# Weight halves made once in block 0 of a decoder step, kept in DRAM, and loaded by the later blocks

## What is computed

```python
h = rmsnorm(x, attn_norm_g)
z = h @ w_in                                   # one projection, split into q,k,v,iq,ik,iw,gq,gk,gv,gr,glr
score = sum_h iw[h] * relu(iq[h] . ik)         # indexer; each query keeps its top-k keys
_, sel = top_k(where(admissible, score, -inf), topk)
a_o = softmax(q . k[sel] / 8 + rel_bias) @ v[sel]
g_o = gated_linear_attention(gq, gk, gv, glr)  # chunked, with its own norm and gate
x = x + concat(a_o, g_o) @ w_out
h = rmsnorm(x, ffn_norm_g)
x = x + (silu(h @ w_gate) * (h @ w_up)) @ w_down
y = rmsnorm(x, final_norm_g)
```

## Time and profile before

| | PE | DVE | ACT | POOL |
|---|---|---|---|---|
| busy us | 3274.2 | 2305.7 | 1701.0 | 1621.3 |
| share | 82% | 58% | 43% | 41% |

### The profile page before, as it was taken

How to read it: one execution, slowest core, us unless ns; L and a number is a source line. 1 busy time by engine, 2 the same in 40 slices (tenths; PEclk the granted TensorE clock), 3 DMA queues, 4 the chain that set the end, 5 groups by cost and what they waited for, 6 DMA issues and landing times.

```text
span 4000.7 us, 56701 instructions
## 1 busy us (share of the span) xinstructions
PE 3274.2 (82%) x19950; PEld 1877.7 (47%) x19950; DVE 2305.7 (58%) x4243; ACT 1701.0 (43%) x2557; POOL 1621.3 (41%) x1232
## 2 busy tenths in 40 slices
PE   4972598899979988999189988999287867899865
PEld 1451346344456543444176543444066653344455
DVE  3625762689934645999843646999977430300155
ACT  0332232554455336544164335644064434554356
POOL 1015200567662035676042034576120113676524
PEclk9995696999989999999599989999699867999856
DMA  2301031223321311233010311233010144233356
GB/s 84 94 25 43 6 99 50 65 95 98 96 86 33 97 66 62 85 93 97 0 64 28 101 58 60 73 96 98 18 35 1 36 159 151 79 97 93 101 190 224
DMA packets 112098, 313.51 MB, mean 78 GB/s; under 512 B 14034, under 2 KB 20514, under 8 KB 111746
## 3 DMA queue, kind: packets, MB, share of 16 engines
q1 hardware_dynamic: 111874, 310.63, 24.6%
HBM read 296.35 MB, written 14.24 MB: 78 GB/s over the span
## 4 chain that ended last, share of the span: by engine, by line
PE 53%; DVE 25%; issue 6%; DMA 4%; ACT 3%; POOLq 3%; DVEq 2%; POOL 2%; PEldq 0%; SPq 0%; ACTq 0%; PEld 0%
PE bank L606 12%; PE bank L607 12%; PE bank L608 12%; DVE spare L1435 11%; PE bank L870 5%; PE bank L859 2%; DVE cand L1451 2%; DVE scores L1491 2%; DVE miss L1448 2%; DVE ring L1405 2%; DMA kT<-in_w_gu 1%; DVE R L1779 1%; POOL H L2063 1%; ACT ring L1059 1%; DVE spare L1470 1%
## 5 line engine op out<-in xcount | busy, mean ns | idle before, releaser
L606 PE MATMUL bank<-H,ring 128*128 128x512 f16 (+2 forms) x2560 | 852.9, 350 | 104.3 <-POOL H L2063 52.9
L607 PE MATMUL bank<-H,ring 128*128 128x512 f16 (+2 forms) x2560 | 853.0, 350 | 0.0
L608 PE MATMUL bank<-H,ring 128*128 128x512 f16 (+2 forms) x2560 | 852.8, 350 | 0.0
L1435 DVE TENSOR_SCALAR_CACHE_REDUCE spare<-scores,cand 128x640 uint8<-128x640 f32 (+8 forms) x448 | 662.3, 1478 | 40.5 <-issue 0.9
L1902 POOL TENSOR_TENSOR ring<-raw,ring 128x1024 f16<-128x1024 f32 (+1 forms) x216 | 407.9, 1895 | 283.2 <-ACT raw L1061 277.5
L1059 ACT ACTIVATE ring<-raw 128x1024 f16<-128x1024 f32 (+2 forms) x356 | 348.7, 980 | 371.0 <-DMA raw<-in_w_d 150.8
L606 PEld LDWEIGHTS bank<-H,ring 128*128 128x128 f16 (+1 forms) x2560 | 257.9, 102 | 370.6 <-issue 101.2
L1405 DVE SCALAR_TENSOR_TENSOR ring<-raw,ring 128x1024 f16<-128x1024 f32 x140 | 198.9, 1424 | 307.7 <-ACT ring L1059 306.7
L608 PEld LDWEIGHTS bank<-H,ring 128*128 128x128 f16 (+1 forms) x2560 | 259.6, 102 | 246.1 <-issue 7.4
L607 PEld LDWEIGHTS bank<-H,ring 128*128 128x128 f16 (+1 forms) x2560 | 258.7, 102 | 236.0 <-issue 4.3
L845 PE MATMUL bank<-kT,q 128*128 128x256 f16 (+3 forms) x384 | 128.8, 340 | 278.6 <-DVE mx L1779 249.6
(11 more groups left out here) (307 smaller groups left out, 6119.8 us busy)
## 6 DMA issues: line engine op xcount, KB each, us to landing
raw<-in_w_gu SPq DMA_DIRECT2D x132, 512.0 KB, 3.6
raw<-in_w_in SPq DMA_DIRECT2D x104, 512.0 KB, 3.5
kT<-in_w_gu SPq DMA_DIRECT2D x88, 512.0 KB, 3.8
raw<-in_w_d SPq DMA_DIRECT2D x48, 384.0 KB, 3.2
X<-in_xT SPq DMA_DIRECT2D x8, 2048.0 KB, 9.1
raw<-in_w_d SPq DMA_DIRECT2D x48, 320.0 KB, 3.4
raw<-in_w_out SPq DMA_DIRECT2D x24, 512.0 KB, 3.7
kT<-in_w_d SPq DMA_DIRECT2D x32, 384.0 KB, 3.2
```

The costliest lines, as they stand in the source:

```text
L606: mm(o, lhs[0], rhs[0], start=first, stop=False)
L607: mm(o, lhs[0], rhs[1], start=False, stop=False)
L608: return mm(o, lhs[1], rhs[0], start=False, stop=last)
L1435: v.tensor_scalar(flags[:, 0:128 * (i + 1)], row_of(i), cut_at[:, i % 4:i % 4 + 1], None, ALU.is_ge, ALU.add, accum_out=tally[:, i % 4:i % ...
```

## The change

P0, O0, U0 and D0 split their weights as before (split_here), but SP stores each pair of halves to a DRAM buffer, split_w, of 107 tiles; a pair of float16 halves has as many bytes as the float32 tile. The save of tile n−2 is issued ahead of the load of tile n, behind the same wait for "w_split", and the last two tiles of P0 and of D0 are saved at the end of the stage (save_rest). highs waits for the save of the tile that had its ring slot before. All tiles of P1 to P4 and of O, U and D in F1 to F4 are loaded from split_w straight into the ring: SP waits for "products" of the tile that had the slot, and PE waits for the load. ACT and the lows of DVE and POOL skip these tiles. There are four slots as before, and from the fifth tile of P4 on eight, the other four in kT. F4's eight O tiles are all loaded in A4 (two before). The U loop of F3 and F4 runs in turns of eight tiles. The diff, cut; left out are the constants, the counting helpers loads_of and saved counts, the index argument added to the other calls of weights, and the U loop on PE, which only follows the turns:

```diff
+        split_w = nc.dram_tensor("split_w", (NW, 128, 2, WT), F16, kind="Internal").ap()
...
+        def split_here(n):
+
+            return n < W_O or base["O", 0] <= n < base["P", 2]
+
+        def raw_no(n):
+
+            return n if n < W_O else n - base["O", 0] + W_O
+
         def raw_at(n):
-
-
-            last = base["P", NBLK] + 4
-            if n < last:
-                return raw[:, n % 2, :], S(f"weights_in{n % 2}"), n // 2, 2
-            m = (n - last) % 4
-            keys = kT[:, :, :, :].rearrange("p g s n -> p (g s n)").bitcast(F32)
-            return keys[:, WT * m:WT * m + WT], S(f"last_weights_in{m}"), (n - last) // 4, 4
+            r = raw_no(n)
+            return raw[:, r % 2, :], S(f"weights_in{r % 2}"), r // 2
+
+        EIGHT = base["P", NBLK] + 4
+        late_ring = kT[:, :, :, :].rearrange("p g s n -> p (g s n)").rearrange("p (m s n) -> p m s n", m=4, s=2)
+
+        def slot_of(n):
+
+            return n % 4 if n < EIGHT or n % 8 < 4 else 4 + n % 4
+
+        def ring_at(n):
+
+            return (ring if slot_of(n) < 4 else late_ring)[:, n % 4, :, :]
+
+        SLOT_USERS = [[n for n in range(at) if slot_of(n) == m] for m in range(8)]
+        USE = {n: k for users in SLOT_USERS for k, n in enumerate(users)}
+
+        def user_before(n):
+
+            k = USE[n]
+            return SLOT_USERS[slot_of(n)][k - 1] if k else None
+
+        def turns(n):
+
+            return 4 if n < EIGHT else 8
...
+            def saved_at(w, i, step):
+
+                if i is None:
+                    return split_w[w]
+                return split_w[bass.ds(i * step + w, 1)].rearrange("t p s m -> p (t s) m")
+
+            def save(n, w, cols, i=None, step=0):
+
+                sp.dma_start(saved_at(w, i, step)[:, :, 0:cols], ring[:, n % 4, :, 0:cols]
+                             ).then_inc(S(f"w_saved{n % 4}"), 16)
+
+            def save_rest(n, w, cols):
+
+                for d in range(2):
+                    sp.wait_ge(S("w_split"), raw_no(n + d) + 1)
+                    save(n + d, w + d, cols[d])
+                for m in range(4):
+                    sp.wait_ge(S(f"w_saved{m}"), 16 * saves_of(n + 1 - (n + 1 - m) % 4))
+
+            def weights(n, src, w, i=None, step=0, saved_cols=WT):
                 cols = src.shape[-1]
-                place, arrived, m, places = raw_at(n)
-                if m:
-
-                    sp.wait_ge(S("w_split"), value(n - places + 1, i, step))
-                sp.dma_start(place[:, 0:cols], src).then_inc(arrived, 16)
+                if split_here(n):
+                    r = raw_no(n)
+                    if r >= 2:
+
+                        sp.wait_ge(S("w_split"), value(r - 1, i, step))
+                    if r >= 2 and r not in (W_O, W_O + 1):
+                        save(n - 2, w - 2, saved_cols, i, step)
+                    place, arrived, _ = raw_at(n)
+                    sp.dma_start(place[:, 0:cols], src).then_inc(arrived, 16)
+                else:
+                    if user_before(n) is not None:
+                        sp.wait_ge(S("products"), value(user_before(n) + 1, i, step))
+                    sp.dma_start(ring_at(n)[:, :, 0:cols], saved_at(w, i, step)[:, :, 0:cols]
+                                 ).then_inc(S(f"halves_in{slot_of(n)}"), 16)
...
+                    if b == 0:
+                        save_rest(W_O - 2, W_O - 2, (WT, WT))
...
-                    for t in range(2):
-                        weights(base["O", b] + t, a["w_out"][t])
+                    for t in range(KT):
+                        weights(base["O", b] + t, a["w_out"][t], W_O + t)
...
+                    turn = turns(base["U", b])
+
+                    def gate_up_weights(count, i=None):
+
+                        for r in range(count):
+                            f = (0 if i is not None else 2 * NF // turn * turn) + r
+                            if i is None:
+                                row = a["w_gu"][f // 2]
+                            else:
+                                row = a["w_gu"][bass.ds(i * (turn // 2) + r // 2, 1)].rearrange("t p m -> p (t m)")
+                            weights(base["U", b] + f, row[:, WT * (r % 2):WT * (r % 2) + WT], W_U + f, i, turn)
+
+                    with sp.Fori(0, 2 * NF // turn) as i:
+                        gate_up_weights(turn, i)
+                    gate_up_weights(2 * NF % turn)
...
+                    if b == 0:
+                        save_rest(base["P", 2] - 2, NW - 2, [128 * len(D_BLOCKS[r]) for r in (2, 3)])
...
-                pe.wait_ge(S("w_split"), value(n + 1, i, step))
-                return ring[:, n % 4, 0, :], ring[:, n % 4, 1, :]
+                if split_here(n):
+                    pe.wait_ge(S("w_split"), value(raw_no(n) + 1, i, step))
+                else:
+                    pe.wait_ge(S(f"halves_in{slot_of(n)}"), value(16 * loads_of(n), i, 16 * step // turns(n)))
+                w = ring_at(n)
...
-                whole, arrived, m, places = raw_at(n)
-                act.wait_ge(arrived, value(16 * (m + 1), i, 16 * step // places))
+                if not split_here(n):
+                    return
+                whole, arrived, m = raw_at(n)
+                act.wait_ge(arrived, value(16 * (m + 1), i, 16 * step // 2))
                 if n >= 4:
                     act.wait_ge(S("products"), value(n - 3, i, step))
+                if saves_of(n) > 1:
+                    act.wait_ge(S(f"w_saved{n % 4}"), value(16 * (saves_of(n) - 1), i, 16 * step // 4))
                 last = A(ring[:, n % 4, 0, 0:cols], whole[:, 0:cols], ACT.Copy, scale=W_UP)
...
             def lows(n, i=None, step=0, cols=WT):
-                dve.wait_ge(S("w_high"), value(n + 1, i, step))
+                if not split_here(n):
+                    return
+                dve.wait_ge(S("w_high"), value(raw_no(n) + 1, i, step))
...
-                if kind == "F" and b == NBLK:
-                    with dve.Fori(0, NF // 2 - 1) as i:
-                        for r in range(4):
-                            lows(base["U", b] + 4 + r, i, 4)
-                    for r in range(ND):
-                        lows(base["D", b] + r, cols=128 * len(D_BLOCKS[r]))
-                    with dve.Fori(0, KT - 1) as i:
-                        for r in range(ND):
-                            lows(base["D", b] + ND + r, i, ND, 128 * len(D_BLOCKS[r]))
...
-                pool.wait_ge(S("w_high"), value(n + 1, i, step))
+                if not split_here(n):
+                    return
+                pool.wait_ge(S("w_high"), value(raw_no(n) + 1, i, step))
```

More of the change, by code:

```diff
@@ L472, in _ @@
                             phase_start(sp, nph)
-                        weights(n0 + t, a["w_in"][t] if t < len(TILES) else a["w_out"][t - len(TILES)])
+                        weights(n0 + t, a["w_in"][t] if t < W_O else a["w_out"][t - W_O], t)
                         if t == 18 and b < NBLK:
@@ L553, in _ @@
                         load_x(b, NT)
-                    for t in range(4 if woven(b) else 2, KT):
-                        weights(n0 + t, a["w_out"][t])
-                    with sp.Fori(0, NF // 2) as i:
-                        for r in range(4):
-                            row = a["w_gu"][bass.ds(i * 2 + r // 2, 1)].rearrange("t p m -> p (t m)")
-                            weights(base["U", b] + r, row[:, WT * (r % 2):WT * (r % 2) + WT], i, 4)
+                    for t in range(4 if woven(b) else 2 if b < NBLK else KT, KT):
+                        weights(n0 + t, a["w_out"][t], W_O + t)
+                    turn = turns(base["U", b])
[10 more added lines that the diff above has]
+                    gate_up_weights(2 * NF % turn)
                     with sp.Fori(0, KT // 2) as i:
@@ L565, in _ @@
                             ks = D_BLOCKS[r % ND]
-                            weights(base["D", b] + r, row[:, 128 * ks[0]:128 * ks[-1] + 128], i, 2 * ND)
+                            weights(base["D", b] + r, row[:, 128 * ks[0]:128 * ks[-1] + 128], W_D + r, i, 2 * ND,
+                                    WT if r < 2 else 128 * len(D_BLOCKS[(r - 2) % ND]))
+                    if b == 0:
+                        save_rest(base["P", 2] - 2, NW - 2, [128 * len(D_BLOCKS[r]) for r in (2, 3)])
                     if b + 2 <= NBLK:
                         for t in range(2):
-                            weights(base["P", b + 2] + t, a["w_in"][t])
+                            weights(base["P", b + 2] + t, a["w_in"][t], t)
                     if b == NBLK - 1:
@@ L994, in _, with up_tiles @@
                     pe.wait_ge(S("f_h"), KT * (b + 1))
-                    def gate_up_loop():
-                        with pe.Fori(0, NF // 2) as i:
-                            for r in range(4):
-                                w = weights_at(base["U", b] + r, i, 4)
-                                pe.wait_ge(S("u_bank_free"), i * 4 + (u0 + r + 1))
-                                for k in range(KT):
```

(20 more changed lines are left out.)

19 lines of the change are left out of this document (13 added, 6 removed).

## The result

The changed kernel takes 3788.11 us (median of four, 3777.9 to 3798.9) against 4003.95 before (median of four); the ratio is 0.945 [0.940, 0.950].

A forecast was written before the change was run, and what follows sets the result against it. Bounds: PE in 512-column matmul stages, DVE's search tail before A2 and A3, and block 4's matmuls and waits for halves. Terms −73 − 47 + 15.5 + 4 − 25 − 38 = −163.5; 4002.9 − 163.5 − 0.5 = 3839 us, range 3805 to 3885.

The forecast's parts named there:

- if PE alone is the bound: Block 4's U4 and D4: the far end of that term, PE's 81 us setting the length, −49 us.
- The search: F1 and F2: without POOL's lows DVE's top-k search steps are no longer stretched, −73 us; ends 30 and 95.
- Rival 2: F1 and F2: POOL's other instructions take over the collisions, the two stages give 30; 3882 us, chance 0.10.
- The lows in the A stages: A0 to A3: DVE's lows waiting for ACT's highs no longer hold up attention, −47 us; ends −25 and −68.
- The saves: Block 0: saves ahead of loads cost +15.5 us, at the start, O0 and D0; ends +5 and +34.
- Rival 3: Block 0: a load moves only after the save before it has landed; 3909 us, chance 0.08.
- The wait in G2 and G3: G2 and G3: store o_v goes out later and POOL waits for it, +4 us; ends 0 and +10.
- O1 and O2, P4, and the way into F3: Lows and splits there go: −2.5 us in each of F1 and F2, −10 in P4, −10 into F3; −25.
- Block 4's F: F4: halves load straight into eight places at 346 GB/s, U4 and D4 −33 us, O4 and A4 −5; −38.
- rival 1: F4 is already at the DMA rate it can have, 265 GB/s; 3865 us, chance 0.15.
- Rival 4: Blocks 1 to 3: with only four ring slots, slow loads of halves hold up PE; 4069 us, chance 0.04.
- Rival 5: Whole kernel: halves are saved but stages stay as long, within 0.2% of before; chance 0.01.

The follow-up runs named there:

- again: The changed kernel, unaltered, measured and profiled once more: 3780.27 us (3775.9 to 3787.1), ratio 0.943 against before.
- a_splits: The changed kernel, with ACT and DVE splitting four tiles of constant data again in each of A1 to A3: whole execution 3812.86 us.
- best: The changed kernel plus early store o_v, block 0 loads ahead of saves, and D tile halves side by side: 3755.38 us, 0.937 against before.
- pool_busy: The changed kernel, with POOL again running an instruction of the old lows' shape on an unneeded buffer in F1 and F2: whole execution 3885.91 us.
- late_store: The kernel before, with store o_v in P2 and P3 made to wait for the product of P's last tile: ratio 0.999 [0.998, 1.001].
- four_slots: The changed kernel with four ring slots to the end instead of eight, four of O4's tiles loaded in A4: whole execution 3814.85 us.

## Why the prediction was wrong

Its mechanisms stood where they were tested, and no term had the wrong sign in both profiles. The spans of the two profiles are 203.6 and 218.6 us shorter than before, so the sum of 163.5 is short by 40 and by 55: nearly every gain was sized short, and some stages were put at nothing.

**The step that failed: PE's own time was held fixed.** The sum took away waits and instructions and left each matmul its old duration, and so it put stages such as G1 at nothing. But for the same matmuls PE's busy time over the whole span fell from 3274 us to 3226, and to 3210 in again, and with it the mean granted clock rose from 0.887 to 0.910 and 0.918. In A3 it rose from 0.91 to 0.95, 8 us less of PE, undone by a_splits with the stops. In G1, put at nothing, it rose from 0.53 to 0.77 and the stage fell by 12.7 us, in again by 7.7; in G4 with I4 PE had 8 us less in the first profile and none in again. In the G stages the clock's part is measured, but that the change made it rise there is not shown.

The clock is not the whole of the shortfall. In the U and D stretches of F1 and F2 it was 1.00 before and after; the search was short by another cause, below. In P4 (0.75 to 0.88, PE busy 34.0 to 28.6 us), U4 (0.69 to 0.93, 51.7 to 40.0) and D4 (0.57 to 0.87, 30.1 to 21.5) it rose as well, but there PE is busy for half to three quarters of the time only, DMA's share is 0.87 in P4 and 0.96 in U4, and D4 grew shorter again when its loads alone ran faster (best): these gains go by the loads, and PE's faster matmuls cannot be added to them. It does make the prediction's bound "if PE alone is the bound" (81 us) too long, of which it had said only "a little more should its clock rise".

**The range.** It took the ends of one term at a time. The prediction's own end of 95 for the search gives 3817, and not the 3807 that it writes; its ends for all terms at once would give about 3765 (an estimate: 4002 less 237), and the 3788 lies inside that. Several terms came out beyond the forecast together.

**The search, −73 forecast, −84.6 measured.** Two thirds of 62 us was too little for L1902: after the change L1546 is stretched by 18 ns and not by 437, so the lows took more of the collisions than my overlay gave them. F1's tail fell by 40.6, the forecast 41 almost to the digit, but by chance: another 9.8 us came out of U, where PE no longer waits for DVE's adds. Those waits stood in the trace before, in the waits of PE in F1, and I read past them:

```profile
PE bank L627 <- DVE scores L1489: 6.4, 3, 2.2
PE bank L627 <- DVE scores L1491: 4.1, 6, 1.1
```

They are 10.5 us, and none is left after. F2 is much the same: −7.6 in U and −26.7 in the tail. What made DVE's adds late is not settled: with POOL's accesses back (pool_busy) these waits in F1 are 1.6 us. Rival 2 (POOL's other instructions take over the collisions) did not come: they collide a little, L1543 stays at 308 ns, but F1 and F2 gave 85 us and not 30. The chain from POOL's accesses over DVE's steps to the tail is shown by pool_busy. The Trainium skill's rule of the shared port pair (SBUF — State Buffer, SBUF: two separate sides) agrees with that experiment as to the cause (L1546 at 179 ns without the accesses and 492 with them); shared out by POOL's busy time it gave 35 us in F1, where 50 were found.

**The lows in the A stages, −47 forecast, −55.5.** A0 −9.2 and A1 −5.7 against 10.5 and 7.5; A2 −9.9 and A3 −30.8 against 7 and 22. Right in mechanism: a_splits undoes it in A1 to A3, though in A1 it does not tell the waits from the work. A3's surplus is the clock; half was too little for A2 and too much for A1.

**The saves, +15.5 forecast, +15.3.** B +2.5, O0 0 and D0 +12.8; in again +2.7, +1.7 and +11.9. The size of D0's term is partly luck: by the 346 GB/s a save of 384 or 320 KB is 1.1 or 0.9 us and not 1.2, and what the loads lost is the 0.7 and 0.8 us of their landing, over 16 turns some 12 us (an estimate) without any lead taken off. Rival 3 (a load waits for a save's landing) is out: D0 did not lose 50 us and U0 did not change. The Trainium skill (DMA: Bandwidth & Descriptors, Two DMAs through the same engine are not ordered) says that descriptors of one queue start in order but are pipelined; U0, 242.0 us before and after, agrees.

**The wait in G2 and G3, +4 forecast, +27.9 and in again +2.8.** The wait is there and of the forecast size, POOL starting 1.9 us later in each of the two than before; the rest of what was measured is the clock, which spreads one G stage of the changed kernels over 20 us from execution to execution. A range made from fixed durations could not hold that: in the two profiles together the three G stages move from −5 to +15 us against before. One profile of before was taken as its level, too. In it G1 stood at 64.8 us, clock 0.53; late_store has 64.9.

**O1 and O2, P4, and the way into F3, −25 forecast, −39.6 and in again −31.7.** O1 and O2 came as forecast, −5.1. P4 gave 14, and four_slots shows that 11 of these came with the eight places and not with the end of the lows, on which I had put it: nearly the size for the wrong reason, and in P4 the depth was not in the sum at all. G4 and I4 lost the three POOL lows and gained 8 us of PE's clock in the first profile, nothing of it in the second.

**Block 4's F, −38 forecast, −47.5 and in again −50.7.** The rate taken, 346 GB/s, is what U4 and D4 reached together (349), and rival 1, which kept them at 265, is out. The term was short because O4 and A4 gave 9 to 12 instead of 5, and because U4 with D4 took 87 us where the forecast had 92.

**Not in the sum: −19.6, in again −16.0.** P0, G0 with I0, P1 and G1, mostly G1 and the clock. The 1.7 us of P1 come in every profile of the changed kernels; the 3.8 of G0 with I0 are no effect of the change that can be told, since late_store has 83.7 us without it and pool_busy 86.7 with it. Rival 4 (four slots are too few) did not come: P2, P3, D1 and D2 keep their length to 0.2 us, so a load lands in time even with four places as long as a tile takes PE 3.6 us or more. Rival 5 (no change in time) is out by the ratio of 0.945.

## What to carry to other kernels

When a change takes stops out of a stage, read the granted clock of that stage and give PE's own time an end at the higher level, where PE and not a load sets the stage's length; in this kernel PE's busy time fell from 3274 to 3226 us for the same matmuls. A wait of a second engine for the first (here PE for DVE's adds) is part of the same loss as the slow instruction behind it, so list every wait that ends on the engine you relieve. And where TensorE is the bound, as in P and the feed-forward stages of 512 tokens, work taken from the other engines counts only through what it disturbs: here 76 us of the gain came from a GpSimd instruction that was itself long hidden.

## What the runs showed of the hardware

- The granted clock of the same 215 matmuls of a G stage differs from execution to execution of one program, 0.56 to 0.90 for G2, and moves the stage between 69.3 and 51.7 us (the changed kernel). No run here told what decides it.
- A GpSimd instruction of 1.85 us in the same memory stretches DVE's two-element steps to 492 to 700 ns on average; without it they take 179 to 308.
- DMA loads into the on-chip memory moved about 368 GB/s with two runs of 1.5 or 1.25 KB per partition and 398 with one run of twice that, all else the same; with runs of 4 KB, U4's loads moved 410 over 33 us:

```profile
DMA packets 3719, 13.53 MB, mean 410 GB/s; under 512 B 415, under 2 KB 415, under 8 KB 3719
```
